# A hybrid decoder step: convolution, level masks, scatter, first dispatch, last pair and final norm rearranged

## The reference

```
p  = rms_norm(x, g_mix) @ w_in                       # 1024 -> 2816 columns
rw = rwkv7(p[:, :1792])                              # token shift, decay/gate projections, recurrence over time, group norm
u  = p[:, 1792:2304] * sigmoid(p[:, 2304:])          # gated unit
cv = silu(layer_norm(depthwise_conv(u, 31 taps)))    # 512 channels, causal, state of 30 rows for the samples
x += concat(rw, cv) @ w_out
x += cross_attention(rms_norm(x), memory keys, values)
t  = rms_norm(x, g_moe); comb = softmax of the top 4 of 32 router logits
for e in 32 experts:
    hid = (clip(t @ w_up[e] + b_up[e]) + 1) * gate * sigmoid(1.702 * gate),  gate = min(t @ w_gate[e] + b_gate[e], 7)
    y  += comb[:, e] * (hid @ w_down[e] + b_down[e])
x += y; result = rms_norm(x, g_final)                # besides it the new shift, convolution, recurrence and memory states
```

## Time and profile before

| what | value |
|---|---|
| time, median of 3 runs | 1436.73 us (1436.44 to 1436.81) |
| the profiled execution | 1443.86 us, of it 1442.1 us span |
| TensorE busy | 1329.6 us (92%) |
| VectorE busy | 406.1 us (28%) |
| ScalarE busy | 201.7 us (14%) |
| GpSimd busy | 25.7 us (2%) |
| DMA | 464.53 MB, mean 322 GB/s over the span |
| mean granted TensorE clock | 0.969 |

### The profile page before, as it was taken

The page is one execution under the profiler, slowest core; times in us unless marked ns, Lnnn a source line. Parts: engine busy times, 40 slices in busy tenths (PEclk is TensorE's granted clock), DMA queues, the critical chain, the costliest instruction groups (busy, mean ns, idle before and its releaser), DMA issues.

```text
span 1442.1 us, 19228 instructions
## 1 busy us (share of the span) xinstructions
PE 1329.6 (92%) x8246; PEld 674.4 (47%) x8246; DVE 406.1 (28%) x834; ACT 201.7 (14%) x354; POOL 25.7 (2%) x42
## 2 busy tenths in 40 slices
PE   6999599889989999999999999999999999999995
PEld 4777596447758533333433433334333333343332
DVE  0368975442022221221121222211212112121221
ACT  2214120032131110000100110001101000010002
POOL 0002200000000000000000000000000000000000
PEclk9999799879999799999999999999999999999998
DMA  6336114208368389999999999999999999999992
GB/s 245 117 124 111 47 33 147 92 29 354 126 262 337 122 337 426 428 429 429 429 429 429 429 428 429 426 429 429 428 429 429 429 429 429 429 428 428 429 429 120
DMA packets 38635, 464.53 MB, mean 322 GB/s; under 512 B 8432, under 2 KB 9008, under 8 KB 10304
## 3 DMA queue, kind: packets, MB, share of 16 engines
q1 hardware_dynamic: 37760, 459.99, 76.8%
q0 software_dynamic: 832, 3.90, 1.2%
HBM read 458.80 MB, written 5.07 MB: 322 GB/s over the span
## 4 chain that ended last, share of the span: by engine, by line
PE 74%; DMA 18%; DVE 4%; ACT 3%; issue 1%; DVEq 0%; ACTq 0%; SPq 0%
PE ps L884 34%; PE ps L467 26%; DMA ring<-in_w_down 17%; PE ps L908 4%; PE ps L1006 4%; DVE arena L1229 2%; PE ps L895 2%; ACT arena L1022 1%; PE ps L913 1%; DVE ring L1226 1%; PE ps L1000 1%; PE ps L862 1%; DVE arena L1226 1%; DMA vec<-in_vec 0%; PE ps L901 0%
## 5 line engine op out<-in xcount | busy, mean ns | idle before, releaser
L884 PE MATMUL ps<-ring,arena 128*64 128x512 f32 x3072 | 688.7, 600 | 20.0 <-DMA ring<-in_w_down 20.0
L884 PEld LDWEIGHTS ps<-ring,arena 128*64 128x64 f32 x3072 | 213.6, 137 | 456.8 <-issue 438.7
L467 PE MATMUL ps<-arena,ring 128*128 128x288 f32 (+2 forms) x1152 | 231.8, 372 | 8.1 <-DVE arena L1229 7.5
L467 PEld LDWEIGHTS ps<-arena,ring 128*128 128x128 f32 (+1 forms) x1152 | 180.3, 177 | 53.9 <-issue 11.9
L1022 ACT ACTIVATE arena<-ps 64x512 f32<-64x512 f32 (+7 forms) x156 | 90.9, 589 | 677.4 <-PE ps L901 328.1
L1229 DVE SCALAR_TENSOR_TENSOR arena<-arena,vec 128x256 f32<-128x256 f32 x248 | 81.9, 406 | 20.5 <-ACT arena L1033 20.4
L1571 DVE TENSOR_SCALAR arena<-ps 128x512 f32<-128x512 f32 x32 | 22.1, 692 | 213.7 <-PE ps L895 213.7
L1553 DVE TENSOR_TENSOR arena<-ps,vec 128x1024 f32<-128x1024 f32 x16 | 19.6, 1225 | 187.2 <-PE ps L913 187.2
L1576 DVE TENSOR_SCALAR arena<-ps 128x512 f32<-128x512 f32 x32 | 22.1, 692 | 177.7 <-PE ps L884 177.7
L908 PEld LDWEIGHTS ps<-arena 128*128 128x128 f32 x512 | 58.4, 192 | 13.0 <-issue 13.0
L467 PE MATMUL ps<-ring,arena 128*32 128x256 f32 (+4 forms) x408 | 60.6, 439 | 2.0 <-ACT arena L1022 2.0
(11 more groups left out here) (203 smaller groups left out, 634.6 us busy)
## 6 DMA issues: line engine op xcount, KB each, us to landing
ring<-in_w_gate SPq DMA_DIRECT2D x64, 2048.0 KB, 22.1
ring<-in_w_up SPq DMA_DIRECT2D x64, 2048.0 KB, 20.6
ring<-in_w_down SPq DMA_DIRECT2D x64, 2048.0 KB, 22.0
ring<-in_w_in SPq DMA_DIRECT2D x5, 2048.0 KB, 8.0
ring<-in_cache_k SPq DMA_DIRECT2D x4, 2048.0 KB, 17.4
ring<-in_cache_v SPq DMA_DIRECT2D x4, 2048.0 KB, 8.0
ring<-in_w_mk SPq DMA_DIRECT2D x2, 2048.0 KB, 8.3
ring<-in_w_mv SPq DMA_DIRECT2D x2, 2048.0 KB, 14.0
```

What stands on the lines that cost most here:

```text
L467: return nc.tensor.matmul(out, lhsT, rhs, start=start, stop=stop)
L884: last = nc.tensor.matmul(out[AT[h ^ swap], :], lhs(k), part(ring, i * SLOT, 4, D)[:, k % 4, h * 512:(h + 1) * 512], start=(fresh and k == ...
```

## The change

It has seven parts.

1. `W_IN_ORDER` begins with the convolution's tiles. VectorE's taps for the prompt are done while TensorE is still in `w_in`, two channel groups at a time; the samples' taps become, for each group, four products of 8 x 31 elements, one reduction and one addition (`conv_sample`). No tap is left in the recurrence.
2. The memory norm's squares follow the first column tile in place of the fourth.
3. The masks of levels 1 to 4 move from GpSimd to VectorE (`mask_level`); the masks of level 0 are made inside the chunk loop.
4. One `dispatch` gathers both experts of the first pair; the biases of `w_down` join the first scatter (`biased`).
5. The scatter of a pair stands behind the gate product of the next pair's expert 0; its additions into `y` are in five parts (`add_up`). VectorE does one of the copies to `ye`.
6. The last pair is written out: no dispatch, the last half of the last `w_down` matrix in four transfers with a semaphore each, the scatter at its end.
7. The final norm (`closing`) works in halves, with `Sqrt` and `reciprocal` in place of `Ln` and `Exp`, and the stores go out in five parts, before the loads are read and the loops left.

Tiles also move within `arena` (`y`, `ye`, `pick`, `h_tok` and others), and `xe` and the temporaries of the gated unit (`gmin`, `sig`, `ug`, `hid`) lie in `xT`'s space, which is read by the first pair's transposes before.

```
-W_IN_ORDER = (12, 13, 4, 5, 6, 7, 14, 18, 15, 19, 16, 20, 17, 21, 0, 1, 2, 3, 8, 9, 10, 11)
+W_IN_ORDER = (14, 18, 15, 19, 16, 20, 17, 21, 12, 13, 4, 5, 6, 7, 0, 1, 2, 3, 8, 9, 10, 11)
...
+        taps_of = [part(arena, at, NB, NT, TAPS) for at in (15544, 16824)]
...
+                        if last and (n, c) == (5, 1):
+                            for k in range(4):
+                                sp.dma_start(ring[:, i * SLOT + k * D:i * SLOT + (k + 1) * D], src[:, k * D:(k + 1) * D]).then_inc(S[f"piece{k}"] if k < 3 else slot_in[i], 16)
+                        else:
+                            sp.dma_start(part(ring, i * SLOT, SLOT), src).then_inc(slot_in[i], 16)
...
-            pool.wait_ge(S["cm_out"], 2 * NC)
-            for l in range(1, len(LEVELS)):
-                flat = "p n c t -> p (n c) t"
-                tell("m_ready", g.tensor_tensor(Mk[l].rearrange(flat), LT[:, 0:NC - 1, :, :].rearrange(flat),
-                                                C("levels")[:, (l + 1) * CH:(l + 2) * CH].unsqueeze(1).broadcast_to([P, (NC - 1) * CT, CH]), ALU.mult), False)
...
+                linear("w_in", n, hT, TOK, range(8), "p_ps", 4 * n, p_reader, 4 if n < 5 else 2, steps=("h_done", 1),
+                       after=lambda m: None if m else squares(2, part(arena, 4352, KT, MEM), MEM, 7))
...
-            pe.wait_ge(S["conv"], CT * TAPS)
+            pe.wait_ge(S["conv"], CT * (TAPS + 1))
...
-            pe.wait_ge(S["pick_ready"], 1)
-            pe.wait_ge(S["htok_ready"], 3)
-            dispatch_one(0, (psT, psU), "disp_done")
...
+                    if pieces and 4 <= k < 7:
+                        pe.wait_ge(S[f"piece{k - 4}"], r * 16 + 16)
+                    elif k == 0 or k == 4 or pieces and k == 7:
+                        pe.wait_ge(slot_in[i], fill * 16 + 16 * (1 + FRONT_FILLS[i]))
...
+            pe.wait_ge(S["pick_ready"], 2)
+            pe.wait_ge(S["htok_ready"], 3)
+            dispatch(psDT)
+            pe.wait_ge(S["small_in"], 16 * 8)
+            pe.wait_ge(S["y_added"], 3)
...
+            def scatter(s, biased=False):
+
+                pe.wait_ge(S["gT_ready"], s + 1)
+                pe.wait_ge(S["ye_ready"], 3 * s + 3)
+                if biased:
+                    pe.wait_ge(S["combT_ready"], 1)
+                for d in range(4):
+                    last = nc.tensor.matmul(psD[TAIL * d:TAIL * (d + 1), 0:256], gT[:, d // 2, SEQ:TOK], ye[d // 2][:, d % 2 * 256:(d % 2 + 1) * 256],
+                                            start=True, stop=not biased, skip_group_check=True)
+                if biased:
+                    for d in range(4):
+                        last = nc.tensor.matmul(psD[TAIL * d:TAIL * (d + 1), 0:256], combT[:, SEQ:TOK], b_down[:, 256 * d:256 * (d + 1)],
+                                                start=False, stop=True, skip_group_check=True)
+                last.then_inc(S["scat_done"], 1)
                 for j in range(2):
                     for h in range(2):
-                        last = mm((psY, psDT)[j][:, h * 512:(h + 1) * 512], combT[:, j * P:(j + 1) * P], b_down[:, h * 512:(h + 1) * 512])
-                    last.then_inc(S["bias_ps"], 1)
-
-            def step(r, q, s):
+                        out = (psY, psX)[j][:, h * 512:(h + 1) * 512]
+                        last = nc.tensor.matmul(out, gT[:, h, j * P:(j + 1) * P], ye[h], start=True, stop=not biased, skip_group_check=True)
+                        if biased:
+                            last = nc.tensor.matmul(out, combT[:, j * P:(j + 1) * P], b_down[:, h * 512:(h + 1) * 512],
+                                                    start=False, stop=True, skip_group_check=True)
+                        last.then_inc(S["scat_done"], 1)
...
+                opening = isinstance(s, int) and first
...
+                pe.wait_ge(S["xe_ready"], r * TURNED + (1 if first else q + 2))
+                multiply(psG, in_xe(0), 0, 2 * s, range(KT), True)
+                if not first:
+                    scatter(s - 1, biased=isinstance(s, int) and s == 1)
                 if opening:
-                    pe.wait_ge(S["xe_ready"], 1)
-                    multiply(psG, in_xe(0), 0, 0, first, True)
-                    pe.wait_ge(S["xe_ready"], 2)
-                    multiply(psG, in_xe(0), 0, 0, second, True)
-                    pe.wait_ge(S["pick_ready"], 2)
-                    pe.wait_ge(S["y_added"], 3)
-                    for i in range(TT):
-                        last = mm(psT[:, 0:NE], first32 if i == 2 else ones, mask[:, i, :], i == 0, i == TT - 1)
-                    last.then_inc(S["pos_ps"], 1)
-                    pe.wait_ge(S["comb_ready"], 1)
-                    for j in range(2):
-                        mm(psU[0:NE, j * P:(j + 1) * P], comb[:, j, 0:NE], ident)
-                    mm(psU[0:NE, SEQ:TOK], comb[0:TAIL, 2, 0:NE], ident[0:TAIL, 0:TAIL]).then_inc(S["combT_ps"], 1)
-                    dispatch_one(1, (psX[:, 0:512], psX[:, 512:]), "disp_done")
-                    down_biases()
-                    pe.wait_ge(S["bias_added"], 1)
-                else:
...
+                pe.wait_ge(S["y_added"], s * PARTS + 3)
...
+                if not last:
+                    pe.wait_ge(S["pick_ready"], r * PICKED + q + 4)
+                    if opening:
+                        pe.wait_ge(S["combT_ready"], 1)
+                    dispatch(psX)
...
+                multiply(psT, in_hT(1), 4, 2 * s + 1, range(KT), True, "down_done", swap=True, r=r, pieces=last)
+                if last:
+                    scatter(s)
...
+            act.wait_ge(S["conv"], CT * (TAPS + 1))
...
+                if last:
+                    a.activation(dummy, eps[:, 0:1], ACT.Sqrt)
+                act.wait_ge(S["down_done"], 2 * s + 1)
+                copy(ye[0][0:CAP], psD[0:CAP])
+                copy(ye[1][CAP:P], psD[CAP:P]).then_inc(S["ye_ready"], 1)
+                act.wait_ge(S["down_done"], 2 * s + 2)
+                copy(ye[0][CAP:P], psT[CAP:P]).then_inc(S["ye_ready"], 1)
...
-            tell("log", a.activation(ssq[:, 0:2], ssq[:, 0:2], ACT.Ln, scale=1.0 / D, bias=eps[:, 0:1]), False)
-            tell("log", a.activation(ssq[:, 2:3], psG[:, 0:1], ACT.Ln, scale=1.0 / D, bias=eps[:, 0:1]))
-            tell("root", a.activation(ssq, ssq, ACT.Exp, scale=-0.5), False)
+                def square(n, x, total):
+                    act.wait_ge(S["y_added"], at + n + 1)
+                    a.activation(unread[n], x, ACT.Square, accum_out=total).then_inc(S["ssq_done"], 1)
...
+                square(0, y_tail, ssq[:, 2:3])
+                for j in range(2):
+                    square(2 * j + 1, y[:, j, 0:512], sq_half[:, 2 * j:2 * j + 1])
+                    act.wait_ge(S["ssq_done"], r * 7 + 3 * j + 2)
+                    a.activation(sq_bias[:, j:j + 1], sq_half[:, 2 * j:2 * j + 1], ACT.Identity, scale=1.0 / D, bias=eps[:, 0:1]).then_inc(S["ssq_done"], 1)
+                    if j:
+                        act.wait_ge(S["tail_ps"], r + 1)
+                        root(ssq[:, 2:3], psG[:, 0:1], eps[:, 0:1])
+                    square(2 * j + 2, y[:, j, 512:D], sq_half[:, 2 * j + 1:2 * j + 2])
+                    act.wait_ge(S["ssq_done"], r * 7 + 3 * j + 4)
+                    root(ssq[:, j:j + 1], sq_half[:, 2 * j + 1:2 * j + 2], sq_bias[:, j:j + 1])
...
+            def conv(cs, lo, hi):
+
+                for k in range(lo, hi):
+                    for c in cs:
                         w = V("dw_w", c * TAPS + k)
+                        xp, yp = ext[:, c, k:k + SEQ], mix[:, CT + c, 0:SEQ]
                         if k == 0:
+                            last = v.tensor_scalar(yp, xp, w, V("dw_b", c), MUL, ADD)
                         else:
+                            dve.wait_ge(S["conv"], taps_done[c])
+                            last = stt(yp, xp, w, yp, MUL, ADD)
+                        tell("conv", last, False)
+                        taps_done[c] = max(taps_done) + 1
+
+            def conv_sample(c):
+                prod, ys = taps_of[c % 2], mix[:, CT + c, SEQ:TOK]
+                w = vec[:, VEC["dw_w"] + c * TAPS:VEC["dw_w"] + (c + 1) * TAPS].unsqueeze(1).broadcast_to([P, NB, TAPS])
+                for t in range(NT):
+                    last = tt(prod[:, :, t, :], ext[:, c, TAPS - 1 + SEQ:].rearrange("p (b t) -> p b t", b=NB)[:, :, t:t + TAPS], w, MUL)
+                link(last)
+                link(v.tensor_reduce(ys, prod.rearrange("p b t k -> p (b t) k"), AX.X, ADD))
+                tell("conv", v.tensor_scalar(ys, ys, V("dw_b", c), None, ADD), False)
+
+            unit(0)
+            unit(1)
             dve.wait_ge(S["pool_i"], 9)
+            dve.wait_ge(S["u_done"], 4)
+            conv((0, 1), 0, 11)
+            unit(2)
+            conv((0, 1), 11, 22)
+            unit(3)
+            conv((0, 1), 22, TAPS)
+            dve.wait_ge(S["p_out"], 4)
+            shift(12, 14)
+            dve.wait_ge(S["u_done"], 8)
```

(43 more changed lines are left out.)

381 lines of the change are left out of this document (158 added, 223 removed).

## The result

The changed kernel takes 1389.81 us in the median of 4 runs (1387.87 to 1390.56), against 1436.77 for the kernel before on the same chip (1436.44 to 1440.45): a ratio of 0.9665, 95% interval 0.9647 to 0.9684. The forecast was 1390.8, with a range of 1383 to 1404. The profiled execution took 1387.87 us, of it 1386.1 us span, at a mean granted clock of 0.988.

A forecast was written before the change was run, and what follows sets the result against it. The weight stream at 428 GB/s, not the 92% busy TensorE, was taken as the bound. Gains of 16.4 + 17.6 + 11.9 = 45.9 us put the profiled execution at 1398.0, less 7.1 for the median: 1390.8 us, range 1383 to 1404.

The forecast's parts named there:

- The frame: Experts' part: time is the gapless stream's start, plus its bytes at 428 GB/s, plus what follows the last landing.
- Part 1: Front, masks and taps: TensorE's 14.7 us stall at the level masks goes, 16.4 us gained, bounds 12 and 18.
- A: Front: VectorE late before `prep`, as prompt instructions wait for the one two back; 12 us more, 1402; 13%.
- D: Front: masks bring too little, VectorE in the chunk loop paces TensorE, half the stall stays; 1399; 3%.
- Part 2: First pair: the 18.0 us pause before the ninth fill goes; 17.6 us gained, bounds 14.1 and 20.5.
- six full slots cover them: Pair 2's scatter: the second gathering and 8.20 us of bias products return there, covered by full slots.
- B: First pair: another wait, some 4 us late, opens the gap again; half of it back is 1400; 7%.
- C: Last matrix: quarters cost 2.7 us each, one after another, so the end is 4.6 us later; 1395; 5%.
- E: Every pair: `add_up` before VectorE's `gate(0)` delays TensorE, pairs over 61.7 us; slower, 1440 or more; 2%.
- The deferred scatter: Every pair: moving the scatter is worth 0 while the stream covers it, about 1.4 us a pair uncovered.
- Part 3: The end: no last `dispatch` 3.6, one copy 0.6, norm by halves 7.7; 11.9 us gained, bounds 8 and 14.
- first pair some 16 us sooner: Sign expected in the changed profile: the experts' first pair comes about 16 us earlier.

The follow-up runs named there:

- masks alone: The kernel before with the masks of levels 1 to 4 moved to VectorE, taps where they were: 1428.31 us, ratio 0.9928.
- masks last: The changed kernel with the masks of levels 1 to 4 back on GpSimd, nothing else: 1392.24 us, ratio 0.9681.
- the kernel with the biases first: The changed kernel with the bias products back in the first pair, ahead of its first up product: 1395.69 us, ratio 0.9706.
- the experiment: The changed kernel with eight useless matmuls of 512 columns ahead of the second pair's first up product: 1401.22 us, ratio 0.9749.
- the second profile of before: The kernel before, unchanged, profiled once more: 1438.54 us in one run, where the first profiled execution took 1443.86.
- the first set: The first runs of the kernel before, on the same chip as the changed kernel's: median 1436.77 us.
- the kernel with the scatter moved: The changed kernel with every pair's scatter and additions back at the end of its own pair: 1394.5 us, ratio 0.9688.
- the eight products in pair 1: The changed kernel with eight useless matmuls between gate and up product of the first pair: 1402.46 us, ratio 0.9747.

## Why the prediction was right, point by point

**The frame held.** Time = start of the stream + bytes at 428 GB/s + what follows the last landing: the last column of the table moves with the pauses of the queue and with the end, to within 1 us.

**Part 1 (16.4).** The levels' end and the recurrence came 17.4 us sooner, the first addition 18.0. Rivals A and D are refuted by the trace: A (VectorE late before `prep`) by taps of 0.40 us and the 3.36 us that VectorE waits, D by the 0.18 us. What I had given to GpSimd (8.6 us of slow taps) and to the old order can't be split: masks alone are worth 10 us, masks last 2.3 by the ratios and 3.7 by the profiles.

**Part 2 (17.6).** The pause of 18.0 us is gone. The first pair brought 2.9 more, since its gate product, at 451.42, took 7.09 us at full clock in place of 9.95; I had this as the upper bound, 20.5. The stream itself gained 17.0, not 18.0: from the seventh fill to the half matrix at 1405.43 it took 922.6 us before, and to that at 1360.65 it takes 905.6. So the part brought 19.9, and 17.6 was too small by the 2.9 us that the clock of the gate product brought, less 0.6. (By its own rows the ninth slot was free at 491.2 to 492.2, not 491.7 to 492.6; nothing hangs on it.) The biases and the second gathering were the pause's cause: the biases alone bring back 7.1 of it. Wrong was the sentence that "six full slots cover them" in pair 2. Six landed slots cover TensorE, not the stream. With the biases in its scatter the stretch from the ninth fill to the twenty-first takes TensorE 61.0 us, without them 54.9 (471.33 to 526.20 in the kernel with the biases first), and its 12 fills last 58.8. The prediction had no term for these 6.1 us. That they cost only 0.4 us by the issues, 0.7 by the bytes, is luck: 1.8 us of fills happened to be queued still. The 12.1 us of the experiment show what anything more there costs.

**Rivals B, C and E.** No other wait opened in the first pair (the ninth fill follows 8.0 us behind the seventh), and quarters cost at most 0.3 us. E was about every pair, and is refuted: from 524.11 to 578.99 TensorE takes 54.9 us of its own, and in the steady part a pair lasts 58.8, the stream's time. Only the stretch with the biases is longer than the stream's, by 2.2 us.

**The deferred scatter ("worth 0 while the stream covers it").** For the steady pairs this holds. Early on it is worth 2.5 us, by the same mistake.

**Part 3 (11.9).** 11.3, and its terms hold one by one. From the last but one half matrix to the end of the last product it takes 12.1 us where it took 15.5: 3.5, forecast 3.6. To the scatter 0.5, forecast 0.6. From the scatter's end to the last multiplication 4.4 in place of 12.3: 7.9, forecast 7.7, of which the norm by halves with its functions is 4.1; the rest, with the loops' exits, has no run of its own. The stores behind it take 0.7 longer.

**The sum.** 45.9 forecast, 47.0 between the medians. It came out as near as that partly by luck, since errors cancel: I worked from a profiled execution that held 7 us of low clock in the samples' stage. By subtracting gains from it and then taking off the 7.1 by which it lay above its median, I removed them unseen. Worked from the second profile of before, which had the clock, the ledger is 50.7 = 19.3 (`w_out` sooner) + 3.2 (from there to the seventh fill, of it 2.0 by the gate product, which took 9.13 us in that profile) + 17.0 (the stream, 922.5 us in that profile) + 11.2 (the end). The front is 2.9 more than my 16.4, and parts 2 and 3 together 1.9 more than my 29.5. After's profiled run lies 1.9 below its median and this one of before 1.8 above the median of the first set: 50.7 - 1.9 - 1.8 = 47.0. The sign "first pair some 16 us sooner" was missed for the same reason: the seventh fill came 27.7 us sooner, with 8.9 of the clock in it.

## What to carry to other kernels

When a stream of weights is the bound, count the fills that are queued, not the slots that are full: queued fills x time of one is the longest that the consumer may hold a slot, and early on, when everything has landed, this cover is at its smallest. Put extra work where the consumer already waits for the stream; there 24 us of it cost nothing that shows here, while 8.8 us in the second pair cost 12, part of it by the half clock that came with them. And price two edits that serve the same stall together: alone, each has another price depending on which comes first.

## What of the hardware was not expected

The same products of the same program ran at 1.02 us each in one execution and 1.92 in another, with the granted clock at 1.0 or 0.50 (2.4 or 1.2 GHz) for up to 24 us. In both cases TensorE had stood idle about 5 us shortly before (4.47 in after and in the kernel with the scatter moved alike), so the idle time before it doesn't decide which. An added hold of TensorE costs more than its length: with 8.8 us of useless work the next fill came 11.9 us later (536.94 - 524.11, less 0.97 of later start), with the granted clock at 0.74 from 520 to 540 us where after had 1.00.

The clock fell there without any idle time of TensorE. Its eight products of 32 rows, in the timeline:

```profile
520.28 8.76 PE L484 MATMUL ps<-arena 32*128 32x512 f32 x16
```

From 526 to 534 us TensorE is busy for all 8 us, with the granted clock at 0.50. The same came with the eight products in pair 1 (0.50 from 470 to 474 us) and with the bias products ahead of the first up product (0.50 from 464 to 470), each time behind a row of products with 32 rows alone. In the scatter of the kernel shown here, where products of 32 and of 128 rows alternate, the clock is 1.00 from 510 to 520. So a busy TensorE is no warrant for the full clock; whether it is the 32 rows that decide, no run here tests.
